# Expert scores computed as the first 16 blocks of the expert stage, with the choices of experts beside them

## The reference, cut to what matters

```python
q = (hn @ w_query).reshape(B, S, PEER_HEADS, 2, PEER_HALF)
s = jnp.einsum('bshpd,hpkd->bshpk', q, sub_keys)
v1, i1 = lax.top_k(s[..., 0, :], PEER_TOPK)
v2, i2 = lax.top_k(s[..., 1, :], PEER_TOPK)
cand = (v1[..., :, None] + v2[..., None, :]).reshape(B, S, PEER_HEADS, PEER_TOPK * PEER_TOPK)
cv, ci = lax.top_k(cand, PEER_TOPK)
expert = e1 * N_KEYS + e2          # e1, e2: i1, i2 taken at ci
gate = jax.nn.softmax(cv, axis=-1)
pre = jnp.einsum('tkd,td->tk', expert_u[expert], x)
act = jax.nn.gelu(pre) * gate
h = h + jnp.einsum('tk,tkd->td', act, expert_v[expert])
```

## Time and profile before

| | |
|---|---|
| median of 3 runs | 4462.69 us (4461.27 to 4474.57) |
| the profiled execution | 4461.64 us, of it 4460.1 us span |
| PE busy | 4089.4 us, 92% |
| DVE, ACT, POOL busy | 2525.6, 1314.9, 2023.3 us (57%, 29%, 45%) |
| score stage, first to last product | 1669 to 1883 us |
| in-blocks | 1903 to 3183 us |
| out-blocks | pass 0 from 3183 us, pass 1 from 3909 us, the last ends near 4447 us |

### The profile page before, as it was taken

The page is one execution under the profiler, slowest core; times in us unless marked ns, Lnnn a source line. Parts: engine busy times, 40 slices in busy tenths (PEclk is TensorE's granted clock), DMA queues, the critical chain, the costliest instruction groups (busy, mean ns, idle before and its releaser), DMA issues.

```text
span 4460.1 us, 55939 instructions
## 1 busy us (share of the span) xinstructions
PE 4089.4 (92%) x19920; PEld 3424.5 (77%) x19920; DVE 2525.6 (57%) x4788; ACT 1314.9 (29%) x1806; POOL 2023.3 (45%) x1384
## 2 busy tenths in 40 slices
PE   6958788888788889989999999999899999999998
PEld 5834378787666567789998998999788888878887
DVE  5453367767313333167767777777544444477774
ACT  2113323232102212133333333333322222243333
POOL 1023132433100000048888888888888888701100
PEclk9979889898889999999999999999999999999999
DMA  2249200000121011256676666667777777789984
GB/s 99 94 165 401 95 17 8 9 16 8 71 89 38 0 61 57 81 160 191 180 196 182 191 191 175 185 180 198 186 189 191 193 191 190 232 279 329 323 283 171
DMA packets 376320, 679.96 MB, mean 152 GB/s; under 512 B 153488, under 2 KB 228240, under 8 KB 358672
## 3 DMA queue, kind: packets, MB, share of 16 engines
q1 hardware_dynamic: 210320, 476.97, 31.6%
q0 software_dynamic: 165888, 201.86, 18.6%
HBM read 526.17 MB, written 152.50 MB: 152 GB/s over the span
## 4 chain that ended last, share of the span: by engine, by line
PE 46%; POOL 7%; issue 2%; DVE 1%; DMA 1%; ACT 0%; DVEq 0%; SPq 0%; POOLq 0%; ACTq 0%
PE peer_ps L2035 27%; PE peer_ps L1994 18%; POOL gates_d L1947 7%; DMA peer_rows<-in_expert_uv,peer_idx 0%; DMA rows<-in_expert_uv,peer_idx 0%; PE peer_ps L2043 0%; POOL peer_rows L1964 0%; POOL rows L1964 0%; DMA late_in<-gates_d 0%; DVE peer_acc L2283 0%; ACT peer_uh L2128 0%; DVE peer_hid L2180 0%; ACT high L2148 0%; SPq L1923 0%; DVEq L2198 0%
## 5 line engine op out<-in xcount | busy, mean ns | idle before, releaser
L1947 POOL DMA_INDIRECT gates_d<-peer_gates,peer_idx x896 | 1540.3, 1719 | 323.7 <-issue 269.2
L1994 PE MATMUL peer_ps<-high,peer_uh 128*128 128x448 f32 x2048 | 587.0, 368 | 30.2 <-DVE low L2186 18.6
L1994 PE MATMUL peer_ps<-low,peer_uh 128*128 128x448 f32 x2048 | 585.8, 367 | 0.0
L1994 PE MATMUL peer_ps<-high,peer_ul 128*128 128x448 f32 x2048 | 585.2, 367 | 0.0
L1994 PEld LDWEIGHTS peer_ps<-high,peer_uh 128*128 128x128 f32 x2048 | 385.0, 189 | 66.8 <-issue 14.4
L1994 PEld LDWEIGHTS peer_ps<-high,peer_ul 128*128 128x128 f32 x2048 | 386.2, 189 | 33.3
L1994 PEld LDWEIGHTS peer_ps<-low,peer_uh 128*128 128x128 f32 x2048 | 386.2, 189 | 33.2
L2297 DVE TENSOR_TENSOR peer_vl<-peer_val,peer_vh 128x1024 fp32r<-128x1024 f32 x171 | 209.5, 1225 | 316.2 <-ACT peer_vh L2109 316.2
L2035 PE MATMUL peer_ps<-peer_vh,peer_ah 128*128 128x512 f32 x1198 | 370.7, 391 | 2.9 <-DVE peer_al L2301 2.9
L2035 PE MATMUL peer_ps<-peer_vh,peer_al 128*128 128x512 f32 x1198 | 370.2, 390 | 0.0
L2035 PE MATMUL peer_ps<-peer_vl,peer_ah 128*128 128x512 f32 x1198 | 369.7, 390 | 0.0
(11 more groups left out here) (438 smaller groups left out, 7404.2 us busy)
## 6 DMA issues: line engine op xcount, KB each, us to landing
peer_val<-in_expert_uv SPq DMA_DIRECT2D x171, 512.0 KB, 3.8
gates_d<-mla_zeros POOLq DMA_DIRECT2D x128, 512.0 KB, 29.6
peer_raw<-in_expert_u SPq DMA_DIRECT2D x128, 512.0 KB, 4.6
hidden_d<-peer_hid SPq DMA_DIRECT2D x128, 448.0 KB
late_in<-in_expert_uv SPq DMA_DIRECT2D x85, 512.0 KB, 3.9
peer_act_in<-hidden_d SPq DMA_DIRECT2D x86, 256.0 KB, 4.2
peer_gat<-gates_d SPq DMA_DIRECT2D x86, 256.0 KB, 4.6
peer_act_in<-hidden_d SPq DMA_DIRECT2D x85, 192.0 KB, 4.3
```

Source lines behind the costliest of these rows:

```text
L1947: pool.indirect_dma_start(gates_flat, bass.IndirectOffsetOnAxis(ap=idx[:, n, k:k + 1], axis=0), gates[:, n, k:k + 1], None, compute_op=ALU ...
L1994: last = nc.tensor.matmul(ps[i][:, a, 0:HD], w[:, cols], x[:, kc, a * HD:(a + 1) * HD], start=(kc == 0 and w is uh[i % 2] and x is high), ...
```

## The change

The score stage is removed and its work becomes blocks 0 to 15 (WT = 16) of the expert stage, in front of the 128 in-blocks; it uses the expert stage's buffers for weights (three instead of two), the fourth PSUM tile for the scores, and buffers for keys, queries and scores that are later overwritten by looked-up rows. The input is still split twice: without rstd for the score blocks, with rstd for the in-blocks. The second split starts when the last score product is done; its first two `scale` steps come before.

The choices start in slot 4 (FIRST_UNIT): one unit a slot until slot 14 (11 units), then, from slot 18 on (slots 16 to 143 are the in-blocks), one unit in three slots: pieces 0 and 1, pieces 2 and 3, piece 4, and piece 5 in the slot where the next unit starts. The last unit ends in slot 177, which is out-block 33 of pass 0. Scatters start with the first unit.

Look-ups are now issued inside the scatters of a unit, one at a time, from the eighth dense unit on (`rows_by`); the ring for the early rows has 8 buffers instead of 9, and a group of two rows comes every 2.5 slots, from in-block 14 on, instead of every 2.6 from 9 on. Of the three input buffers of the out-blocks two now lie where `high` lay, so only out-block 0 is loaded before the in-blocks end (before: 0 and 1); out-block 1 is loaded right after them, then h for both passes and the gain, then out-block 2. `SPARSE` is 1: one tile stays looked up.

```diff
+EARLY_SLOTS, PASS_SLOTS = 88, 0
+RING_IN, RING_OUT = 8, 6
-EARLY_SLOTS = 88
-RING_IN, RING_OUT = 9, 6
+WT = 2 * PH
+FIRST_UNIT = 4
...
-    return ([(head, tile) for head in range(PH) for tile in (0, DENSE, 1, 2, 3)]
+    return ([(head, tile) for head in range(PH) for tile in tuple(range(DENSE, NT)) + PASSES[0]]
             + [(head, tile) for head in range(PH) for tile in PASSES[1]])
...
+def unit_pieces():
+
+
+    at, slot = {}, FIRST_UNIT
+    for n in range(UNITS):
+        steps = ((0, 1, 2, 3, 4), (5,)) if slot < WT - 1 else ((0, 1), (2, 3), (4,), (5,))
+        for i, pieces in enumerate(steps):
+            at.setdefault(slot + i, []).extend((n, piece) for piece in pieces)
+        slot += len(steps) - 1
+        if slot == WT - 1:
+            slot = WT + 2
+    return at
...
+        val = [st.sb("val", [P, D])] + [x[:, 0:D] for x in late_in]
+        act_in = [st.sb("act_in", [P, HALF])] + [x[:, D:D + HALF] for x in late_in]
+        gat = [st.sb("gat", [P, HALF])] + [x[:, D + HALF:2 * D] for x in late_in]
...
+        def ahead(b):
+
+            return {WT + NK - 1: 0}.get(b)
...
         def group_slot(g):
 
             if g < EARLY_SLOTS // GROUP:
-                return 9 + (g * 13) // 5
-            return 2 * NK + 2 + 5 * (g - EARLY_SLOTS // GROUP)
+                return WT + 14 + (g * 5) // 2
+            return OUT + NK + 2 + 5 * (g - EARLY_SLOTS // GROUP)
...
+        def rows_by(i, k):
+
+            if i < 7:
+                return 0
+            if i < 31:
+                return EARLY_SLOTS * ((i - 7) * TOPK + k + 1) // (24 * TOPK)
+            return EARLY_SLOTS + (PASS_SLOTS * ((i - 32) * TOPK + k + 1) // ((len(dense) - 32) * TOPK) if i > 31 else 0)
...
+            def store_scores(j):
+                sp.wait_ge(s_ready, j + 1)
+                sp.dma_start(by_head[j // 2, :, j % 2], s[j % 2][:, :, :]).then_inc(w_stored[j % 2], 16)
...
-                if q == 2:
-                    sp.wait_ge(mm_done, NK)
+                if q == 1:
+                    sp.wait_ge(mm_done, WT + NK)
...
+            sp.dma_start(keys[:, :, :], keys_d).then_inc(keys_ready, 16)
             load_raw(2)
+            sp.dma_start(h_d.rearrange("k p t -> p k t"), h[:, :, :]).then_inc(h_stored, 16)
+            for b in range(WT):
+                load_raw(b + 3)
+                if b >= 2:
+                    store_scores(b - 2)
+                if b == FIRST_UNIT - 1:
+                    load_scores(0)
+                    load_scores(1)
+                next_scores(b)
...
+                if c < 2:
+                    store_scores(WT - 2 + c)
+                next_scores(WT + c)
-                if c == NK - 4:
+                if c == NK - 3:
                     load_out(0)
-                    load_out(1)
+            load_out(1)
+            for slot in (OUT, OUT + 1):
+                next_scores(slot)
             for p, tiles in enumerate(PASSES):
                 sp.wait_ge(h_stored, 16)
                 sp.dma_start(rest[p][:, :, 0:len(tiles) * P],
                              h_d[:, :, tiles[0] * P:tiles[-1] * P + P].rearrange("k p t -> p k t")
                              ).then_inc(rest_ready[p], 16)
-            sp.wait_ge(x_low, KC)
+            sp.wait_ge(x_low, 2 * KC)
             sp.dma_start(gain[:, :], fin_row.broadcast_to([P, D])).then_inc(gain_ready, 16)
             for q in range(2, 2 * NK):
...
+                if p < EARLY_SLOTS and p >= RING_IN:
+                    pool.wait_ge(row_used, p - RING_IN + 1)
+                if p == EARLY_SLOTS:
+                    pool.wait_ge(mm_done, WT + NK)
+                if p >= EARLY_SLOTS + RING_OUT:
+                    pool.wait_ge(row_used, p - RING_OUT + 1)
...
+            for i, n in enumerate(dense):
                 head, tile = units[n]
                 pool.wait_ge(idx_ready, n + 1)
                 if scatters(head - 1, tile):
                 for k in range(TOPK):
                     pool.indirect_dma_start(gates_flat, bass.IndirectOffsetOnAxis(ap=idx[:, n, k:k + 1], axis=0),
                                             gates[:, n, k:k + 1], None, compute_op=ALU.add).then_inc(added[tile % 4], 16)
+                    for p in range(turn, rows_by(i, k)):
                         look_up(p)
-                    turn = upto
-            for p in range(EARLY_SLOTS, SLOTS):
+                    turn = max(turn, rows_by(i, k))
+            for p in range(turn, SLOTS):
...
+            for b in range(WT):
+                pe.wait_ge(u_low, b + 1)
+                if b >= 2:
+                    pe.wait_ge(w_taken, b - 1)
+                product(b)
+                if b:
+                    scores(b - 1)
+            scores(WT - 1)
             for i in range(4):
-                pe.wait_ge(u_low, i + 1)
...
+            def score_copy(j):
+                act.wait_ge(s_mm, j + 1)
+                if j >= 2:
+                    act.wait_ge(w_stored[j % 2], 16 * (j // 2))
+                nc.scalar.activation(s[j % 2][:, :, :], ss, ACT.Copy).then_inc(s_ready, 1)
...
+            for b in range(1, WT):
+                high_in(b + 1)
+                score_copy(b - 1)
+                gates_exp(b)
+            x_highs(1)
+            high_in(WT + 1)
+            score_copy(WT - 1)
...
+            gates_exp(OUT)
+            for q in range(1, 2 * NK):
+                row_gelu(OUT + q)
+                gates_exp(OUT + q)
...
+            for b in range(1, WT):
+                take(b - 1)
+                low_in(b + 1)
+                for n, piece in pieces_of(b):
+                    choose(n, piece)
+            scale(0, 1)
+            scale(1, 1)
+            take(WT - 1)
             for kc in range(KC):
-                if kc + 1 < KC:
-                    scale(kc + 1)
-                low_x(kc)
-            low_in(1)
+                low_x(kc, 1)
+                if kc + 2 < KC:
+                    scale(kc + 2, 1)
+            low_in(WT + 1)
...
+            for n, piece in pieces_of(OUT):
+                choose(n, piece)
+            for q_out in range(1, 2 * NK):
+                multiply(q_out)
+                lows_out(q_out)
+                for n, piece in pieces_of(OUT + q_out):
                     choose(n, piece)
```

More of the change, by code:

```diff
@@ L1767, in peer_stage @@
     units = unit_order()
-    looked_up = [n for n, (head, tile) in enumerate(units) if tile == DENSE]
+    pieces_at = unit_pieces()
+    looked_up = [n for n, (head, tile) in enumerate(units) if tile >= DENSE]
+    OUT = WT + NK
     with Stage(nc, "peer") as st:
@@ L1862, in rows @@
             return late_rows[i % RING_OUT], late_ready[i % RING_OUT], i // RING_OUT + 1
+        dense = [n for n, (head, tile) in enumerate(units) if tile < DENSE]
+        def rows_by(i, k):
[4 more added lines that the diff above has]
+            return EARLY_SLOTS + (PASS_SLOTS * ((i - 32) * TOPK + k + 1) // ((len(dense) - 32) * TOPK) if i > 31 else 0)
         @block.sync
@@ L1997, in block_in, with product @@
                 last.then_inc(mm_done, 1)
-            def token_rows():
+            def product(b):
+                i = b % 2
+                for kc in range(KC):
+                    if b == 0:
+                        pe.wait_ge(x_low, kc + 1)
+                    cols = slice(kc * P, kc * P + P)
+                    for w, x in ((uh[i], high), (uh[i], low), (ul[i], high)):
+                        for a in range(2):
+                            last = nc.tensor.matmul(ps[i][:, a, :], w[:, cols], x[:, kc, a * HALF:(a + 1) * HALF],
+                                                    start=(kc == 0 and w is uh[i] and x is high),
+                                                    stop=(kc == KC - 1 and w is ul[i]))
+                    if b == 0 and kc in (3, 5, 7):
+                        sum_squares((kc - 3) // 2)
+                    if b == 1 and kc == 1:
+                        sum_squares(3)
+                last.then_inc(mm_done, 1)
@@ L2334, in _ @@
             nc.vector.tensor_copy(identr[:, :], consts["ident"][:, :])
-            scale(0)
             low_in(0)
+            for kc in range(KC + 1):
+                if kc < KC:
+                    scale(kc, 0)
+                if kc:
+                    low_x(kc - 1, 0)
+            low_in(1)
+            dve.wait_ge(std_ready, 1)
+            nc.vector.reciprocal(rstd[:, :], rstd[:, :]).then_inc(rstd_ready, 1)
+            dve.wait_ge(rstd_ready, 1)
+            for b in range(1, WT):
[3 more added lines that the diff above has]
+                    choose(n, piece)
@@ L2346, in _ @@
                     choose(n, piece)
-                row_hidden(c)
-                row_sums(c)
-                if ahead(c) is not None:
-                    multiply(ahead(c))
-                    lows_out(ahead(c))
-            for q in range(2, 2 * NK):
-                if q == NK + RING - 1:
+                row_hidden(WT + c)
+                row_sums(WT + c)
+                if ahead(WT + c) is not None:
```

(2 more changed lines are left out.)

370 lines of the change are left out of this document (180 added, 190 removed).

## The result

The changed kernel takes 4438.5 us (median of 5 runs, 4426.29 to 4440.6) where the kernel before takes 4462.69 in the same comparison (4460.08 to 4483.06): ratio 0.9928, 95% interval 0.9902 to 0.9955. It is faster by 0.7%; the forecast was 4447, in a range of 4428 to 4471. A second comparison gave 4432.44 against 4463.66, ratio 0.9932 (0.9913 to 0.9952).

A forecast was written before the change was run, and what follows sets the result against it. PE (TensorE) was taken to set the time from the score stage to the end. Terms -13.8 - 23.6 + 3.5 + 18 = -15.9 on 4461.64 gave 4445.7; with the median 1.05 above, 4447 us, range 4428 to 4471.

The forecast's parts named there:

- Score blocks: Score blocks before the in-blocks: choices added on VectorE beside the same matmuls, and the moved h store, cost 0.
- Second split: From last score product (E) to end of in-block 0: E+23.1 against 36.9, -13.8 us, bounds -11 to -16.
- In-blocks: In-blocks up to the end of the last (P): waits for looked-up rows and their stalls go, -23.6 us, bounds 0 to -23.6.
- Hand-over: In-blocks to out-blocks: one MB more to load, out-block 2 starts at P+27 instead of P+23.6, +3.5 us, bounds 0 and +8.
- Choices in pass 0: Out-blocks 0 to 33: PE waits for VectorE, 14 us in ten triples plus 4 for late loads, +18, bounds 0 and +40.
- Pass 1: Pass 1 of the out-blocks: scatters end near 3848, before the gates' load is due near 3862, so 0.
- A: Out-blocks of pass 0: VectorE's triple takes 16.5 us or less, choices cost 0; 4429 us, chance 0.12.
- B: Out-blocks of pass 0: loads late as well, choices cost +40 us; 4469 us, chance 0.15.
- C: In-blocks keep their loss through other stalls or a 9.92 us pace throughout; 4471 us, chance 0.13.
- D: Pass 1 waits for gates as scatters slow beside busy VectorE, deciding from 2.11 us each; at 2.25, 4499 us; chance 0.07.
- E: Out-blocks of pass 0: pauses in each triple make PE's clock fall, ten times 2 us; 4467 us, chance 0.05.

The follow-up runs named there:

- 6: Changed kernel with look-ups spread over 30 or 27 units of scatters instead of 24: in-blocks 12.4 us longer with 30, nothing lost with 27.
- 3: Changed kernel with look-ups in a burst of 3 or 4 after each unit's 16 scatters: no stretch differs by more than 0.3 us.
- 4: Kernel before with look-ups spread between the scatters: last score product to last Gelu 1299.09 us against 1299.72.
- experiment 1: Changed kernel with a unit of choices in two in-block slots, so none lies in pass 0: median 4434.98 us.
- 5: Changed kernel, first scatter held until four in-blocks are done, 2.75 look-ups a unit: last score product to last Gelu 1315.42 us, 51.8 more.
- experiment 2: Changed kernel with h loaded beside out-blocks 48 to 63 and the gain at 72: 2773.70 us from the first score matmul to the end.

## Why the prediction was right

The forecast was 15.9 us less, the profile shows 20.1 less, and the medians 24.2. The median, 4438.5, lies in the stated range; the profiled execution, with the earliest start of all, is 1.7 us below it. By the terms:

1. *Score blocks, 0.* Measured 0.05 less. Right.
2. *Second split, -13.8.* Measured -12.5 in the first profile (E+24.4) and -14.0 in the second (E+22.9). The steps were right, but the forecast had all pairs at the upper clock level, 2.4 GHz. With pauses of 1.03 us before each chunk the clock fell to the lower one for some of them (mean 0.82), and the last chunk at that level cost 1.5 us. Nine of the eleven executions of the changed kernel and its variants end block 0 at E+24.4, two at E+22.9.
3. *In-blocks, -23.6.* Measured -23.6: 1239.2 us from the end of block 0 to P, with TensorE busy in all 1040 us of the window. The reason holds too: GpSimd waits for the ring, VectorE no longer for rows. (The prediction read 25.9 us of waits for rows before; with the second row of that view they were 49.5.) Taking the full value rested only on knowing of no other late input, and it came true. What ended the waits is a pace of look-ups at least as fast as the schedule's: 24 and 27 units lose nothing and 30 lose 12.4 us, with nothing else changed (6). It is neither the way in which look-ups lie between scatters (3, 4) nor three slots a unit (1). The early start let GpSimd scatter seven units before the first look-up, so that 88 rows could go into 24 units. A late start at the old pace brings the waits back (5), but that run changes both. A late start at a quick pace wasn't run, nor was the schedule's own shift (rows from in-block 14 on instead of 9) taken alone, so their shares are not known.
4. *Hand-over, +3.5.* Pass 0 up to block 42 is 15.9 us longer than before; experiment 1 takes 13.5 of it away with the choices, which leaves 2.4. Out-block 2 is split at P+22.8, that of before at P+20.65. Its first matmul came at P+25.7, where 27 were forecast. The forecast had charged the loss to one more MB in the transfers. The chain shows 5.95 us at the issue of the gain's load, which it didn't name; but SyncE stood 5.52 us at the same load in the kernel before, so this is not what made the hand-over longer. What did was not isolated.
5. *Choices in pass 0, +18.* The triple was right, 18.0 us against 17.9, and so was the reason, PE waiting for the second operand's split. Experiment 1 measures 13.5 for all ten. This is the term that was mis-sized, by 4.5 us: the 4 us for late loads did not come. Together with 1.1 too much in term 4 and 1.3 too little in term 2 it makes the difference between forecast and profile (15.9 + 4.5 + 1.1 - 1.3 = 20.2). Ten triples at 1.58 us over TensorE's 16.5 would be 15.8; where the other 2.3 were covered was not followed.
6. *Pass 1, 0.* Measured 0.1. The last scatter ended near 3852.5 (forecast 3848), and pass 0 at 3873.5 (timeline of TensorE, the last of its h added at 3871.56, 1.95 us). It is right by a narrow margin: with 8 to 13 us less in pass 0 the gates became the bound, at a price of 10.5 to 12.5 (1, 2). The forecast put it at nothing from the time at which the scatters end, and this held.

The remaining 4 us between profile and medians may lie in the part ahead of the first score matmul, which scatters by 15 us; this stays open.

Of the rivals, *A* (choices fit) fell with the triple of 18.0 us, *B* (loads late as well) with the same number, as late loads would have made it longer, and *C* with the even 9.73 us. *D*, slower scatters beside a busy VectorE, was looked at where VectorE is busiest. Windows after, scatters alone (POOL busy, count, clock, DMA share, GB/s):

```profile
3131.00:3340.00 209.00, 176.98 (x106) 0.97 0.76 200
3340.00:3840.00 500.00, 426.16 (x243) 1.00 0.75 194
```

A scatter took 176.98 / 106 = 1.67 us with VectorE 88% busy for most of the time and 426.16 / 243 = 1.75 with it at 45%, one every 1.97 and 2.06 us. Neither mean reached 2.11. The rule of the Trainium skill, "SBUF — State Buffer", section "SBUF: two separate sides", by which VectorE's instructions on both ports lock GpSimd out of writing descriptors, would make the first number the larger if the choices use both ports. Which of their instructions do, no view here shows, and the first number is the smaller: this trace doesn't show the rule for these choices and scatters. *E*, the clock: it did not fall in pass 0. The window with the choices has 0.99, and from 3176 us on, when the hand-over is behind, 1.00, although TensorE stood up to 0.96 us before a block in each triple. The swing that the Trainium skill, "TensorE: Matmul & The Clock Gate", section "A second HAM failure mode: psum-queue depth-cycling", describes did not appear at these idles. But it appeared in the second split, at the very pauses of 1.03 us that the prediction had held against E (term 2).

## What to carry to other kernels

A producer that runs at a fixed pace beside a consumer's schedule should be set to that pace. Here a pace too slow made the consumer wait at the end (30 units), and one too quick made the producer stand at its ring and be late with its other work (24 units). When a saving doesn't show in the time, look at the next wait further on, and take both away at once: three edits that gave nothing each alone (two slots, h later, 27 units) gave 0.5% together. Measure from the last instruction that both kernels share, as the part before it can scatter more than the effect.

## What the runs showed of the hardware

- The part that both kernels share, up to the first score matmul, took 1653.6 to 1669.0 us in 13 executions, and most of this scatter goes with TensorE's clock in an earlier stage. Windows 420 to 480 us, first of the kernel before, then of the changed one:

```profile
420.00:480.00 60.00, 53.47 (x188) 28.00 (x188) 17.12 (x50) 15.90 (x32) 8.21 (x15) 0.80 0.84 328
```

```profile
420.00:480.00 60.00, 52.16 (x225) 28.09 (x224) 21.26 (x59) 19.77 (x40) 8.02 (x15) 1.00 0.84 329
```

  The same code has 188 matmul records at a mean granted clock of 0.80 (between the two levels) and 225 at 1.00 (the upper level, 2.4 GHz, throughout). Over 420 to 520 us the 13 executions fall into three kinds: mean clock 0.85 in three, 0.88 in five, 1.00 in five, with variants of the changed kernel in each. They reach the next stage (the first matmul of L946) at 541 to 543, near 538 and at 528 to 530 us, and the first score matmul at 1665.0 to 1669.0, 1660.8 to 1664.8 and 1653.6 to 1658.6. What decides which kind an execution is, no run shows.
- TensorE's clock fell in the second split although no pause there was longer than 1.03 us: pairs of 448 columns went from 0.67 to 1.04 us (mean granted clock 0.82 in the first profile, 0.90 in the second). At pauses of up to 0.96 us before two of every three out-blocks it stayed at 1.00.
- The same small load (the gain, one row spread over all partitions) held SyncE for 5.95 us at its issue when it stood right behind the loads of h, 5.52 us in the kernel before, and 0.44 us in experiment 2, issued at out-block 72 with h loaded before. So the cost goes with what stands ahead in the queue, not with the load itself.
